# Gate/up expert weights in four transfers of two interleaved row blocks, instead of eight of one

## The reference

```python
logits = (hf @ w_router).astype(f32) + b_router
top_logits, top_idx = lax.top_k(logits, TOP_K)          # 4 of 32 experts for each token
top_w = jax.nn.softmax(top_logits, axis=-1)
...
def expert_block(args):
    xb, e = args                                         # rows of tokens sent to expert e
    gu = xb @ w_gate_up[e] + b_gate_up[e]                # 1024 -> 2048, gate and up interleaved
    gate = jnp.minimum(gu[:, ::2], SWIGLU_LIMIT)
    up = jnp.clip(gu[:, 1::2], -SWIGLU_LIMIT, SWIGLU_LIMIT)
    act = (up + 1.0) * (gate * jax.nn.sigmoid(gate * SWIGLU_ALPHA))
    return act @ w_down[e] + b_down[e]                   # 1024 -> 1024
```

## Time and profile before

| | before |
|---|---|
| median of 3 executions | 2272.29 us |
| lowest, highest | 2269.2, 2274.46 us |
| profiled execution, its own time | 2274.53 us |
| span of its trace | 2272.7 us |
| TensorE busy | 2094.5 us, 92% |
| VectorE, ScalarE, GpSimd busy | 23%, 16%, 10% |
| bytes read from HBM | 478.73 MB |

### The profile page before, as it was taken

How to read it: one execution, slowest core, us unless ns; L and a number is a source line. 1 busy time by engine, 2 the same in 40 slices (tenths; PEclk the granted TensorE clock), 3 DMA queues, 4 the chain that set the end, 5 groups by cost and what they waited for, 6 DMA issues and landing times.

```text
span 2272.7 us, 42062 instructions
## 1 busy us (share of the span) xinstructions
PE 2094.5 (92%) x17668; PEld 1066.8 (47%) x17668; DVE 513.5 (23%) x859; ACT 364.6 (16%) x631; POOL 232.8 (10%) x261
## 2 busy tenths in 40 slices
PE   7998898898898799999499999999999999999991
PEld 5467567667667644444233343343343344344340
DVE  1435325335335300022211011011011011011014
ACT  3222322322322300001010010010010010010001
POOL 0012012012012000000301110110110110110110
PEclk8999999999999999999599999999999999999996
DMA  6010010020000331103489999999999999999955
GB/s 232 19 70 10 19 69 9 2 73 22 0 0 0 119 147 74 74 7 144 179 341 387 375 391 383 375 399 393 377 395 388 382 390 394 384 389 388 384 210 200
DMA packets 76134, 488.31 MB, mean 215 GB/s; under 512 B 13492, under 2 KB 14152, under 8 KB 22944
## 3 DMA queue, kind: packets, MB, share of 16 engines
q1 hardware_dynamic: 67392, 470.96, 53.5%
q0 software_dynamic: 8704, 16.82, 2.2%
HBM read 478.73 MB, written 17.45 MB: 218 GB/s over the span
## 4 chain that ended last, share of the span: by engine, by line
PE 89%; DVE 4%; ACT 2%; issue 1%; DMA 1%; DVEq 1%; ACTq 1%; POOL 0%; SPq 0%; POOLq 0%
PE ps L469 32%; PE ps L808 29%; PE ps L826 15%; PE ps L644 6%; DVE arena L1127 2%; ACT arena L877 1%; DVE arena L1130 1%; PE ps L837 1%; PE ps L793 1%; PE ps L803 1%; PE ps L686 1%; PE ps L679 1%; PE ps L819 1%; PE ps L527 1%; DMA arena<-expert_rows 0%
## 5 line engine op out<-in xcount | busy, mean ns | idle before, releaser
L808 PE MATMUL ps<-arena 128*32 128x512 f32 x6144 | 667.3, 594 | 0.0
L808 PEld LDWEIGHTS ps<-arena 128*32 128x32 f32 x6144 | 184.5, 110 | 464.8 <-issue 458.6
L826 PE MATMUL ps<-arena,hT 128*32 128x256 f32 x6144 | 339.3, 381 | 0.0
L469 PE MATMUL ps<-hT,arena 128*128 128x512 f32 x752 | 334.4, 603 | 1.1 <-ACTq L1028 1.1
L877 ACT ACTIVATE arena<-ps 128x1024 f32<-128x1024 f32 (+7 forms) x164 | 109.4, 668 | 957.5 <-PE ps L793 697.1
L826 PEld LDWEIGHTS ps<-arena,hT 128*32 128x32 f32 x6144 | 185.2, 111 | 142.3 <-issue 2.4
L469 PE MATMUL ps<-arena 128*128 128x128 f32 (+3 forms) x864 | 229.5, 409 | 22.7 <-ACTq L979 18.2
L1516 DVE TENSOR_SCALAR arena<-ps 128x768 f32<-128x768 f32 x32 | 30.6, 958 | 953.1 <-PE ps L808 953.1
L469 PEld LDWEIGHTS ps<-hT,arena 128*128 128x128 f32 x752 | 144.4, 194 | 176.4 <-issue 176.4
L469 PEld LDWEIGHTS ps<-arena 128*128 128x128 f32 x864 | 133.8, 193 | 98.8 <-issue 63.5
L1615 POOL DMA_INDIRECT expert_rows<-hT,six x96 | 95.7, 997 | 812.5 <-ACT hT L877 765.7
(11 more groups left out here) (191 smaller groups left out, 1160.3 us busy)
## 6 DMA issues: line engine op xcount, KB each, us to landing
arena<-in_w_gu SPq DMA_DIRECT2D x256, 1024.0 KB, 8.0
arena<-in_w_dn SPq DMA_DIRECT2D x128, 1024.0 KB, 6.9
arena<-in_w_pair SPq DMA_DIRECT2D x16, 1024.0 KB, 4.8
arena<-in_w_merge SPq DMA_DIRECT2D x8, 2048.0 KB, 7.7
arena<-expert_rows SPq DMA_DIRECT2D x3, 2048.0 KB, 13.6
arena<-in_x SPq DMA_DIRECT2D x8, 512.0 KB, 10.3
arena<-in_w_out SPq DMA_DIRECT2D x2, 2048.0 KB, 11.1
arena<-in_w_qb SPq DMA_DIRECT2D x4, 768.0 KB, 4.2
```

What stands on the lines that cost most here:

```text
L469: ins = pe.matmul(dst, lhsT, rhs, start=(k == 0), stop=(k == len(pairs) - 1))
L808: ins = pe.matmul(gu[32 * j:32 * (j + 1), g, :], xT[:, k, 32 * g:32 * (g + 1)], ring[k][:, 512 * j:512 * (j + 1)], start=False, stop=(k == ...
L826: ins = pe.matmul(yd[32 * j:32 * (j + 1), g, 0:256], aT[:, g, k, 32 * c:32 * (c + 1)], ring[8 + c][:, D * k + 256 * j:D * k + 256 * (j + 1 ...
```

## The change

The ring's gate/up part becomes four chunks of twice the size, at the same addresses. Chunk c holds rows 256c to 256c+255; partition p gets rows 256c+2p and 256c+2p+1, which are adjacent in memory, so each partition's share is one run of 16 KB. There are four transfers of 2 MB for each expert instead of eight of 1 MB, each issued when both halves of its chunk have been used. TensorE waits for a chunk once for every two values of k. Since half k % 2 of chunk k // 2 now holds the rows 256(k // 2) + 2p + k % 2, the tokens have to be transposed to match: transpose k takes every second column out of 256 columns of `xg`, beginning with column k % 2 of them. The matmul instructions keep their number, shapes and order. The down weights keep their form, and only their chunk numbers change.

```diff
-        ring = [ar(2 * c, 2 * K1) for c in range(12)]
+        ring = [ar(4 * c, 4 * K1) for c in range(4)] + [ar(16 + 2 * c, 2 * K1) for c in range(4)]
...
         def w_gu_chunk(e, c):
-            return w_gu[bass.ds(e, 1), P * c:P * (c + 1), :].rearrange("o p f -> p (o f)")
+            return w_gu[bass.ds(e, 1), 2 * P * c:2 * P * (c + 1), :].rearrange("o (p k) f -> p (o k f)", k=2)
...
             def up_weights(n, e, chunks):
                 for c in chunks:
                     if not first(n):
-                        sp.wait_ge(gu_used, 8 * n + (c + 1 - 8))
+                        sp.wait_ge(gu_used, 4 * n + (c + 1 - 4))
                     sp.dma_start(ring[c], w_gu_chunk(e, c)).then_inc(chunk_in[c], 16)
...
-            up_weights(0, 0, range(6))
+            up_weights(0, 0, range(3))
...
-            up_weights(0, 0, range(6, 8))
+            up_weights(0, 0, range(3, 4))
...
             def token_columns(n):
                 pe.wait_ge(gathered, 16 * n + 16)
                 for k in range(KD):
                     at = 512 * (k // 4) + ROWS * (k % 4)
-                    ins = pe.transpose(tr[:, at:at + ROWS], xg[0:ROWS, k * P:(k + 1) * P], ident[0:ROWS, 0:ROWS])
+                    ins = pe.transpose(tr[:, at:at + ROWS], xg[0:ROWS, 2 * P * (k // 2):2 * P * (k // 2 + 1)].rearrange("p (m k) -> p k m", k=2)[:, k % 2, :],
+                                       ident[0:ROWS, 0:ROWS])
                 ins.then_inc(xt_done, 1)
...
                 for k in range(KD):
-                    pe.wait_ge(chunk_in[k], 16 * n + 16)
+                    if k % 2 == 0:
+                        pe.wait_ge(chunk_in[k // 2], 16 * n + 16)
                     for g in range(QUADS):
                         for j in range(4):
+                            at = 2 * D * (k % 2) + 512 * j
                             ins = pe.matmul(gu[32 * j:32 * (j + 1), g, :], xT[:, k, 32 * g:32 * (g + 1)],
-                                            ring[k][:, 512 * j:512 * (j + 1)], start=False, stop=(k == KD - 1))
-                    ins.then_inc(gu_used, 1)
+                                            ring[k // 2][:, at:at + 512], start=False, stop=(k == KD - 1))
+                    if k % 2:
+                        ins.then_inc(gu_used, 1)
```

More of the change, by code:

```diff
@@ L307, in build @@
         gu_used, dn_used, bias_clear = sem("gu_used"), sem("dn_used"), sem("bias_clear")
-        chunk_in = [sem(f"chunk_in_{c}") for c in range(12)]
+        chunk_in = [sem(f"chunk_in_{c}") for c in range(8)]
         bias_gu_in, bias_dn_in, ones3_done = sem("bias_gu_in"), sem("bias_dn_in"), sem("ones3_done")
@@ L323, in w_gu_chunk @@
         def w_gu_chunk(e, c):
-            return w_gu[bass.ds(e, 1), P * c:P * (c + 1), :].rearrange("o p f -> p (o f)")
+            return w_gu[bass.ds(e, 1), 2 * P * c:2 * P * (c + 1), :].rearrange("o (p k) f -> p (o k f)", k=2)
         def w_dn_chunk(e, c):
-            kk = c - 8
+            kk = c - 4
             return w_dn[bass.ds(e, 1), 2 * P * kk:2 * P * (kk + 1), :].rearrange("o (p k) f -> p (o k f)", k=2)
@@ L389, in up_weights @@
                     if not first(n):
-                        sp.wait_ge(gu_used, 8 * n + (c + 1 - 8))
+                        sp.wait_ge(gu_used, 4 * n + (c + 1 - 4))
                     sp.dma_start(ring[c], w_gu_chunk(e, c)).then_inc(chunk_in[c], 16)
             def down_weights(n, e):
-                for c in range(8, 12):
+                for c in range(4, 8):
                     if not first(n):
-                        sp.wait_ge(dn_used, 4 * n + (c - 7 - 4))
+                        sp.wait_ge(dn_used, 4 * n + (c - 3 - 4))
                     sp.dma_start(ring[c], w_dn_chunk(e, c)).then_inc(chunk_in[c], 16)
@@ L400, in up_bias @@
                 if not first(n):
-                    sp.wait_ge(gu_used, 8 * n + (1 - 8))
+                    sp.wait_ge(gu_used, 4 * n + (1 - 4))
                 sp.dma_start(bcur[0:3, 0:2 * DE], bias_dram[bass.ds(e, 1), :, 0:2 * DE].rearrange("o b f -> (o b) f")).then_inc(bias_gu_in, 16)
@@ L423, in _ @@
                 sp.dma_start(tab[32 * j:32 * (j + 1), :], slot_dram.rearrange("(p c) o -> p (c o)", p=32)).then_inc(tab_in, 16)
-            up_weights(1, 1, range(8))
+            up_weights(1, 1, range(4))
             up_bias(1, 1)
             with sp.Fori(2, NE) as e:
-                up_weights(e, e, range(8))
+                up_weights(e, e, range(4))
                 up_bias(e, e)
@@ L438, in _ @@
                         e = sp.value_load(lst[0:1, bass.ds(j + LIST, 1)], min_val=0, max_val=NE - 1)
-                        up_weights(j + NE, e, range(8))
+                        up_weights(j + NE, e, range(4))
                         up_bias(j + NE, e)
@@ L821, in down @@
                 for c in range(4):
-                    pe.wait_ge(chunk_in[8 + c], 16 * n + 16)
+                    pe.wait_ge(chunk_in[4 + c], 16 * n + 16)
                     for k in range(2):
@@ L826, in down @@
                                 ins = pe.matmul(yd[32 * j:32 * (j + 1), g, 0:256], aT[:, g, k, 32 * c:32 * (c + 1)],
-                                                ring[8 + c][:, D * k + 256 * j:D * k + 256 * (j + 1)], start=False, stop=(c == 3 and k == 1))
+                                                ring[4 + c][:, D * k + 256 * j:D * k + 256 * (j + 1)], start=False, stop=(c == 3 and k == 1))
                     ins.then_inc(dn_used, 1)
@@ L1512, in expert @@
             def expert(n):
-                dv.wait_ge(gu_used, 8 * n + 8)
+                dv.wait_ge(gu_used, 4 * n + 4)
                 g2 = gu.rearrange("p g (f two) -> p two (g f)", two=2)
```

## The result

The changed kernel takes 2281.97 us (median of six, 2280.36 to 2288.73), against 2272.32 us (2269.20 to 2274.46) for the kernel before. The ratio is 1.0049, with a 95% interval from 1.0036 to 1.0062, so it is slower by 8 to 14 us. The forecast was 2283.2 us, 10.9 us slower. A second comparison, on another chip, gave 1.0063 (1.0048 to 1.0078).

What follows compares the result with a forecast made beforehand. TensorE's instruction stream was taken as the bound, the DMA rate following it. Thirty groups at 0.36 us plus 0.1 made 10.9 us, added to 2272.3 for 2283.2 us; range 2271 to 2289.

Steps and rivals of the forecast that it cites:

- The strided load: Tokens' transposes at L793: weight loads of about 209 ns instead of 141, making the kernel slower; chance 0.78.
- The stage: Transposes up to the bias matmuls: the group of eight takes 1.17 us instead of 0.81, 0.36 us more.
- The pace alone: Low price for a group of eight token transposes: only the interval between loads grows, 0.27 us.
- the sum of all loads: High price for a group of eight token transposes: every load's extra 0.068 us laid end to end, 0.54 us.
- The rule of the Trainium skill: Rival at the token transposes: two hits per 16-byte line suffice, so the stride is free; 2272.3 us, chance 0.12.
- The late refill: Gate/up refills start one chunk later, with 28.7 us of room for a landing of 16.0 us; hidden by matmuls.
- the rival of a late gather: Token gather landing beyond its 15.7 us of room: 2322 us; chance 0.05, shared with late weights.
- late weights: Rival at the expert weights: they arrive too late for TensorE; chance 0.05, shared with the late gather.
- The faster one: Rival: less full DMA engines or fewer waits speed TensorE, at most 2.5 us at the loop's ends; 2269.8 us, chance 0.05.
- issued about one period ahead: Down weights and biases on SP's queue: same order behind the gate/up transfers, still issued a period early; no cost given.
- the wait of 4.1 us for VectorE: Behind block 1's token transposes: this wait swallows the group's delay, so that group adds nothing.
- block 0's group: First block's token transposes, on the path at the lower clock: 0.1 us taken, between 0 and 0.54.

## Why the prediction was right, and what it missed

**What bounds the kernel.** TensorE's stream of one expert set the pace before and after. The DMA share of 0.98 was a rate that followed: with packets of twice the size it went to 0.96, with the stride and without it, and no measurable time came of it. The runs with the larger transfers alone, and with both costs removed, show this at periods of 33.89 and 33.90 us.

**The strided load.** L837 gave the right price for L793 before L793 was strided: 209 ns forecast, 216 measured. The stage was priced at 1.17 us and took 1.13, so the term was 30 x 0.36 = 10.8 and should have been 30 x 0.32 = 9.6 us. Most of the excess sits in the first transpose: the 0.93 us of L837 contain the time from its first matmul to its second, which is 0.22 us there and 0.20 at the strided L793. The pace alone (0.27 us) was too low, the sum of all loads (0.54) far too high. The rule of the Trainium skill ("Advanced Engine Details and Errata", section "SBUF Cachelines"), weighed as a rival at 0.12, is not what the runs show: two elements to a line of 16 bytes are not free, and one to a line costs no more than two.

**The late refill.** The landing of a gate/up transfer went from 8.0 to 9.2 us (median of 128, at most 18.0), against room of 28.7 us. The gather lands after 10.2 us and at most 11.4, where 8.9 and 9.9 had been and 13.8 was the bound; its room of 15.7 us was never used up. So the rival of a late gather fell, and with it that of late weights. The faster one fell with the time itself. (The landing of 4.0 us, which the prediction gives to the first gather, is the second one's, 4.02 us; the first took 4.2. Nothing hangs on it.)

**What was missed.** The main step that failed is the sentence that the down weights and the biases are "issued about one period ahead". It holds for 30 blocks. For the second, nothing lies between the two `up`s but transposes, and the bias was already issued only 5.9 us ahead of its use in the kernel before and landed 1.1 us ahead of it: just in time, and so in no list of waits. With transfers of twice the size ahead of it it came 4.85 us late, and the lower clock level behind the idle time added about 0.9 us more. A row could have shown it, since the issue of L402 at 1148.39 and the start of L803 at 1154.25 both stand in the trace of before; I had looked at the first blocks for the transposes only. By the runs with it alone (ratio 1.0020) and without it (1.0042 against 1.0063) the wait costs 4.5 to 5 us.

Two smaller steps failed too. The prediction let the wait of 4.1 us for VectorE swallow the delay of block 1's group. That wait only starts when ScalarE has what the transposes wrote, so it moved with them, and the 0.32 us were paid: 5.34 us with the stride (five traces), 5.02 without it (four traces; the two kernels with reordered activations have 5.15 and 5.16). And block 0's group, priced at 0.1 us, cost 0.01.

**The sum.** 9.6 for the 30 groups, 0.3 for that of block 1, 4.85 for the wait and 0.9 for the clock make 15.7 us by mechanisms. The loop of the two traces shows 14.9 us, with 1.1 us given back at its end, as far as is known by chance. The forecast said 10.9. The two comparisons measured 11.1 (8 to 14) and 14.3 (11 to 18) us. The forecast lies well in the first interval and at the lower edge of the second; a part of its closeness is thus luck, as an overpriced stride (10.9 in all against 9.9) and the scatter of the executions made up for some of a wait that was not forecast. The direction and the main mechanism were right.

## What to carry to other kernels

Before a load of the stationary operand is given a stride to suit a data layout, look whether the program has such a load already: its row tells the price, which here was 0.04 us per transpose, paid in every period of the engine that sets the pace. When a transfer is made larger, ask of every small one queued behind it how long before its use it is issued, at the first and the last turn of the loop above all; one that is just in time shows in no list of waits. And when one engine waits for the result of another, look what that other one waits for: a wait swallows a delay only if it does not itself begin with the delayed work. A DMA share of 0.98 said nothing on the bound here, as the engine that uses the weights never waited for them.

## What the hardware showed that I had not expected

- In the transposes, a load of 128 columns of float32 takes 140 to 141 ns where they are adjacent, at 96 and at 128 partitions. Where they are not, it takes 209 ns (128 partitions, every second column), 216 (96, every second) or 218 (96, every fourth). This holds for transposes alone: the loads of L679, 128 adjacent float32 columns for an ordinary matmul, take 192 ns (median). Strided loads followed one another every 0.120 us whatever was streamed behind them (96 or 128 columns), while adjacent ones followed the matmuls: every 0.083 us at 96 columns, every 0.109 us at 128.
- A transfer of 12 KB, issued right behind 2 MB that were queued behind another 2 MB, landed 11.0 us after its issue (11.7 with the larger transfers alone); behind transfers of 1 MB it landed after 4.8 us in the kernel before, and 4.6 with the stride alone. In every run that issued a bias ahead of the large transfers, that bias was not waited for.
- At the second block, idle times of 4.1 to 4.3 us were followed by 3.4 us at the lower clock level (eight traces). Where a further 4.85 to 5.76 us of idle time came, it was 10.2 us (three traces: the changed kernel twice, and its transfers alone).
